# Where the modulation sums accumulate, when the token weights are turned, and when the queue asks for weight slots

## The chip, the core and the metric

The program runs on one NeuronCore of a Trainium2 chip. TensorE (PE in the rows) multiplies, VectorE (DVE), ScalarE (ACT) and GpSimd (POOL) do elementwise work, and SyncE (SP) issues most of the DMAs, one after the other: a DMA whose wait isn't met holds every DMA behind it in that queue. The metric is the device time of one execution, in microseconds, lower is better. Work on the chip is held in SBUF (128 partitions) and in eight PSUM banks of 128 x 512 fp32, which TensorE writes and VectorE and ScalarE may read and write.

## The reference, cut to what matters

A sequence of 512 tokens of width 1024 goes through two layers of a first block and then through a second block of two layers (retention, then differential attention), which the change doesn't touch. One layer of the first block is

```
mod = silu(c) @ w_ada + b_ada               # 6 x 1024: shifts, scales, gates
h   = x * (1 + sc1) + sh1
proj = h @ w_in                             # qa ka va | iq ik iw | cq ckv kr | ga gb
scores[q, s] = sum over 8 heads of iw[q, h] * relu(iq[q, h] . ik[s] / 8), causal
sel  = the 128 best keys of each query by scores
ya   = softmax over sel of (qa . ka / 8 + t5 bias) times va          # "DSA attention"
yb   = causal softmax attention on low-rank q, k, v built from cq, ckv, kr   # "MLA attention"
y    = (sigmoid(ga) * (ya @ w_branch_a) + sigmoid(gb) * (yb @ w_branch_b)) @ w_out
x    = layer_norm(alpha * x + g1 * y); then a gated conv feed-forward, g2, layer_norm
```

Everything is fp32. A projection is three matmuls, with the operands split into a high and a low part (w_hi, w_lo; h_hi, h_lo).

## The kernel before, in words

There is no scheduler: each engine's program is written out by hand, and semaphores order them. Weights come in slots of 128 x 2048 fp32 (1 MB). For slot n, SP loads `w_raw[n % 2]` once slot n-2 has been split (`weights`, L421 to L424), ScalarE rounds it into `w_hi` (`split_hi`, L1141 to L1144), GpSimd subtracts to give `w_lo` (L526, four pieces of 512 columns) and posts `w_ready`. TensorE waits for `w_ready` before the slot's tiles. So SP, ScalarE and GpSimd each pass the slots in order, and a late one delays the rest.

A layer of the first block begins with the index stage. TensorE computes tiles 0 to 7 of the projection (slots 0 to 3: four tiles of iq, then tile 4 with ik, kr and iw, then cq and ckv), turns the 8 x 512 token weights `iw_row` by four small transposes (L792), and goes through twelve pairs of heads (`PAIRS`, L803): two score matmuls (L809) into two of banks 4 to 7, then 15 or 18 matmuls of the gate tiles (`BESIDE[2]`, L601 to L603). ScalarE applies the relu in place (L1320), VectorE adds the two heads into `sel` (L1860, L1863). Pair u's scores wait until VectorE has done pair u-2 (L805). VectorE has other work between: the roots' reciprocals and the norm of cq and ckv (L1866 to L1871), the rotation of kr (L1842 to L1844, after a DMA on SP has swapped its halves, L463), and the modulation sums.

The modulation sums ("ada") are a vector times a matrix. Per layer, 16 slices of w_ada of 1 MB each come through a ring of two buffers `ada_mid`. Slice k is asked for in SP's queue between the weight slots, and its DMA waits until slice k-2 is used up. A number is two slices: eight instructions on VectorE, each one adding a scaled 128 x 512 piece to a sum in SBUF (`ada_acc_early`; L1614 and L1616 in `ada_halves`, L1630 and L1636 in `ada_step_at`). Numbers 4 to 6 stand before the pairs, number 7 to 11 lie in pieces within them (40 steps over 12 pairs). After the fourth tile of the next projection TensorE sums the partitions by 64 one-column matmuls (`ada_group`, L628 to L633).

MLA attention follows: 32 units (4 query blocks x 8 heads) with gate tiles between. VectorE does in each unit a logit pass, a scaling, and some steps of the top-k: a step finds the 8 largest of a row (L1751) and strikes them out (L1752), 16 rounds per query block. Block 1 and 2 (256 and 384 keys) are spread over the units, block 3 (512 keys) runs in a loop (L1738, L1741) after them, under the q, k and v projections (8 tiles and 2 slots). Then VectorE makes `yb_lo` (L1729), which TensorE awaits before DSA attention (L680).

DSA attention has the same 32 units. The bias of unit u, 128 x n, is loaded by SP (L480) once unit u-4's logits are done (four buffers), and between the units TensorE works on the branch tiles (`BESIDE[0]`). The four branch slots 20 to 23 are asked for right behind the biases of units 0 to 3. ScalarE's program is: split slot 20, copy the v tiles, split slot 21 (L1364), then the units' exponentials (L1219).

## Time and profile before

| | |
|---|---|
| median of 3 runs | 2768.3 us (2756.35 to 2777.46) |
| profiled execution | 2764.49 us, span 2762.7 us, mean granted TensorE clock 0.940 |
| PE busy | 2537.8 us, 92% of the span, 11130 matmuls |
| DVE, ACT, POOL busy | 1284.0 (46%), 1085.5 (39%), 1011.0 (37%) us |
| index stage, layer 0 and 1 | 138 to 216 us and 1035 to 1110 us of the span |
| MLA attention with its pairs of tiles | 248 to 338 us and 1143 to 1232 us |
| DSA attention | 404.7 to 498.4 us and 1298.7 to 1407.6 us |

Times within the span count from its start. "Busy" of an engine includes work that runs at the lower of the two clock levels; the granted clock says which (1.00 is 2.4 GHz, 0.50 is 1.2 GHz).

### The profile page before, as it was taken

How to read it: one execution, taken by the hardware profiler on the slowest of the kernel's cores; microseconds unless marked ns; L12 is line 12 of the kernel's file. 1: busy time of each engine (PE TensorE's matmuls, PEld its weight loads, DVE VectorE, ACT ScalarE, POOL GpSimd, SP SyncE). 2: the span in 40 equal slices, each digit the busy share in tenths (PEclk: the TensorE clock that was granted, in tenths of full speed). 3: DMA queues.
4: the chain of work that ended last, by engine and by line, in shares of the span. 5: the costliest groups of instructions: out<-in, count | busy, mean ns of one | idle time of the engine just before them, and what ended most of it. 6: DMA issues, size and time to landing. Idle time of an engine off the chain costs nothing.

```text
span 2762.7 us, 32442 instructions
## 1 busy us (share of the span) xinstructions
PE 2537.8 (92%) x11130; PEld 1959.7 (71%) x11132; DVE 1284.0 (46%) x2520; ACT 1085.5 (39%) x1752; POOL 1011.0 (37%) x792
## 2 busy tenths in 40 slices
PE   6989999889999989999988999997999989799877
PEld 4657875667888866787666788884788768577645
DVE  7675735464435478573356434225310160425472
ACT  5443533354443244443233544324223342323662
POOL 2234240244445553424015344454444434244211
PEclk9998997999999989899588999998999999899988
DMA  6642122112235354213121222222223302122100
GB/s 246 215 174 84 47 83 79 67 61 91 91 102 205 105 196 178 69 47 99 46 69 64 76 105 91 89 94 78 77 90 103 130 1 76 48 89 89 64 1 31
DMA packets 51727, 259.11 MB, mean 94 GB/s; under 512 B 6112, under 2 KB 16096, under 8 KB 26016
## 3 DMA queue, kind: packets, MB, share of 16 engines
q1 hardware_dynamic: 50464, 249.26, 26.2%
q0 software_dynamic: 1152, 8.39, 0.8%
q8 instruction: 67, 1.10, 0.2%
q14 instruction: 44, 0.36, 0.0%
HBM read 249.11 MB, written 7.34 MB: 93 GB/s over the span
## 4 chain that ended last, share of the span: by engine, by line
PE 62%; issue 17%; POOL 8%; DVE 8%; ACT 2%; DMA 2%; SPq 0%; DVEq 0%; POOLq 0%; ACTq 0%
PE bank L601 17%; PE bank L602 17%; PE bank L603 17%; POOL w_lo L526 7%; PE bank L690 2%; PE bank L714 1%; PE bank L998 1%; PE bank L703 1%; PE bank L927 1%; PE bank L632 1%; POOL x L547 1%; DMA ada_early<-w_ada 1%; PE bank L1071 1%; DVE ada_acc_early L1636 1%; DMA ada_mid<-w_ada 1%
## 5 line engine op out<-in xcount | busy, mean ns | idle before, releaser
L526 POOL TENSOR_TENSOR w_lo<-w_raw,w_hi 128x512 fp32r<-128x512 f32 (+1 forms) x700 | 916.5, 1340 | 1491.2 <-ACT w_hi L1144 937.1
L601 PE MATMUL bank<-h_hi,w_hi 128*128 128x512 f32 x1792 | 736.7, 411 | 71.2 <-DVE h_lo L1673 35.3
L603 PE MATMUL bank<-h_hi,w_lo 128*128 128x512 f32 x1792 | 708.6, 395 | 0.0
L602 PE MATMUL bank<-h_lo,w_hi 128*128 128x512 f32 x1792 | 708.2, 395 | 0.0
L601 PEld LDWEIGHTS bank<-h_hi,w_hi 128*128 128x128 f32 x1792 | 343.4, 192 | 173.7 <-issue 85.6
L602 PEld LDWEIGHTS bank<-h_lo,w_hi 128*128 128x128 f32 x1792 | 343.8, 192 | 75.2 <-issue 8.4
L603 PEld LDWEIGHTS bank<-h_hi,w_lo 128*128 128x128 f32 x1792 | 342.4, 191 | 74.1
L1926 DVE SCALAR_TENSOR_TENSOR cv<-bank,par,cv 128x511 f32<-128x511 f32 (+1 forms) x176 | 131.8, 749 | 245.7 <-ACT cv L1389 232.8
L1144 ACT ACTIVATE w_hi<-w_raw 128x2048 fp32r<-128x2048 f32 (+1 forms) x108 | 189.5, 1754 | 135.9 <-PE bank L603 128.6
L1149 ACT ACTIVATE w_hi<-w_raw 128x2048 fp32r<-128x2048 f32 x76 | 145.0, 1907 | 35.8 <-PE bank L603 35.8
L1219 ACT ACTIVATE L<-L,nmax 128x128 f32<-128x128 f32 (+3 forms) x128 | 71.9, 562 | 201.8 <-DVE nmax L1690 201.2
L601 PE MATMUL bank<-u_hi,w_hi 128*128 128x512 f32 x352 | 137.9, 392 | 0.0
L602 PE MATMUL bank<-u_lo,w_hi 128*128 128x512 f32 x352 | 137.0, 389 | 0.0
L603 PE MATMUL bank<-u_hi,w_lo 128*128 128x512 f32 x352 | 137.0, 389 | 0.0
L1389 ACT ACTIVATE cv<-bank,par 128x512 f32<-128x512 f32 x88 | 68.5, 778 | 145.8 <-PE bank L603 145.8
L601 PE MATMUL bank<-w_hi,h_hi 128*128 128x512 f32 x256 | 100.4, 392 | 0.0
L603 PE MATMUL bank<-w_hi,h_lo 128*128 128x512 f32 x256 | 99.6, 389 | 0.0
L602 PE MATMUL bank<-w_lo,h_hi 128*128 128x512 f32 x256 | 99.6, 389 | 0.0
L1687 DVE TENSOR_TENSOR bank<-bank,bias_in 128x128 f32<-128x128 f32 (+3 forms) x64 | 31.9, 498 | 143.7 <-PE bank L690 131.8
L2000 DVE TENSOR_TENSOR wt<-bank,decay 128x512 f32<-128x512 f32 (+3 forms) x32 | 13.5, 482 | 171.8 <-PE bank L987 171.8
L1971 DVE TENSOR_TENSOR rt<-bank,rope 128x512 f32<-128x512 f32 x32 | 22.1, 691 | 127.7 <-PE bank L927 112.5
L1199 ACT ACTIVATE ytmp<-bank,mod 128x512 f32<-128x512 f32 x32 | 22.0, 688 | 147.4 <-PE bank L603 147.4
(322 smaller groups left out, 4005.4 us busy)
## 6 DMA issues: line engine op xcount, KB each, us to landing
w_raw<-w_stream SPq DMA_DIRECT2D x150, 1024.0 KB, 4.8
ada_mid<-w_ada SPq DMA_DIRECT2D x32, 1024.0 KB, 5.5
w_raw<-w_down SPq DMA_DIRECT2D x32, 704.0 KB, 4.0
ada_early<-w_ada POOLq DMA_DIRECT2D x8, 1024.0 KB, 8.4
ada_late<-w_ada SPq DMA_DIRECT2D x8, 1024.0 KB, 6.1
bias_in<-bias_scratch SPq DMA_DIRECT2D x16, 256.0 KB, 2.6
bias_in<-bias_scratch SPq DMA_DIRECT2D x16, 192.0 KB, 2.3
x<-x SPq DMA_DIRECT2D x1, 2048.0 KB, 12.8
```

What stands on the lines that cost most here:

```text
L526: ins = nc.gpsimd.tensor_tensor(w_lo[r][:, part], w_raw[r][:, part], w_hi[r][:, part].bitcast(fp32), ALU.subtract)
L547: nc.gpsimd.tensor_tensor(x[:, f, :], x[:, f, :], ln_mean[:, :], ALU.subtract).then_inc(zs_ready, 1)
L601: nc.tensor.matmul(out, w[0][:, cols], xh, start=first, stop=False)
L602: nc.tensor.matmul(out, w[0][:, cols], xl, start=False, stop=False)
L603: return nc.tensor.matmul(out, w[1][:, cols], xh, start=False, stop=last)
L690: nc.tensor.matmul(banks[4 + t % 2][:, 0:n], q[rows, hh, i * P:(i + 1) * P], kk[rows, hh, 0:n], start=True, stop=True).then_inc(s_done, 1)
L1144: A_(w_hi[n % 2][:, 0:cols], w_raw[n % 2][:, 0:cols], ACT.Copy).then_inc(w_hi_done, 1)
L1149: A_(w_hi[n % 2][:, :], w_raw[n % 2][:, :], ACT.Copy).then_inc(w_hi_done, 1)
L1219: A_(L[t % 3][:, 0:n], L[t % 3][:, 0:n], ACT.Exp, bias=nmax[:, t:t + 1], scale=-1.0, accum_out=esum[:, t:t + 1]).then_inc(exp_done, 1)
L1389: A_(cv[s][c][:, :], banks[(t + c) % 4][:, :], ACT.Identity, bias=b, scale=w2).then_inc(conv_first, 1)
L1687: chain(V.tensor_tensor(ps, ps, bias_in[t % 4][:, 0:n], ALU.add))
L1926: return V.scalar_tensor_tensor(out, banks[(t + c) % 4][:, 0:S - 2 + w], weight, out, ALU.mult, ALU.add)
```

## The change

Four edits, in both layers (the kernel's number for a slot, a slice or a unit is used throughout):

1. The ada sums are built up in a PSUM bank (7 outside the pairs, 3 within them and in the feed-forward of layer 0); the last of the eight instructions writes the total to SBUF. Number 7 moves ahead of the pairs, so 32 steps lie within them. Bank 3 is freed by putting the three root sums into bank 2 one after the other, and TensorE's fourth q tile, which writes bank 3, waits for the last sum. The slices are asked for at other places of SP's queue.
2. The token weights are turned between tiles 5 and 6; the rotation of kr moves behind pair 1, the two reciprocals to pairs 3 and 5, and ScalarE takes a pair's relu before a gate tile's sigmoid.
3. SP asks for the branch slots behind the biases of units 3, 5, 7 and 12 instead of all four behind unit 3's.
4. The top-k of block 2 runs in the loop after MLA attention, ahead of block 3's.

```diff
--- before.py
+++ after.py
@@ -450,7 +450,7 @@
                 for m in range(SLOT_IDX, SLOT_GB + 1):
                     if l or m >= 2:
                         weights(l, m, a["w_ukv"][l] if m == SLOT_UKV else ws[m - (m > SLOT_UKV)])
-                    for _ in range((0, 2, 0, 2, 2, 2, 0, 2, 2, 3, 1)[m]):
+                    for _ in range((0, 2, 0, 1, 2, 3, 1, 2, 2, 2, 1)[m]):
...
@@ -479,9 +479,9 @@
                     n = (i + 1) * P
                     sp.dma_start(bias_in[u % 4][:, 0:n], bias_dram[h, i * P:(i + 1) * P, 0:n]
                                  ).then_inc(bias_full[u % 4], 16)
-                    if u == 3:
-                        for m in range(SLOT_BR, SLOT_OUT):
-                            weights(l, m, ws[m - 1])
+                    if u in (3, 5, 7, 12):
+                        m = SLOT_BR + (3, 5, 7, 12).index(u)
+                        weights(l, m, ws[m - 1])
...
@@ -786,29 +786,35 @@
                 first_slot(l, SLOT_IDX, TILE_IDX, h_hi, h_lo, h_ready, KD * hidx(l, 0))
                 for m in range(1, 4):
                     slot_tiles(l, SLOT_IDX + m, TILE_IDX + 2 * m)
+                    if m == 2:
+                        pe.wait_ge(kr_ready, l + 1)
+                        for b in range(NB):
+                            ins = nc.tensor.transpose(banks[4][:, b * H:(b + 1) * H], iw_row[:, b * P:(b + 1) * P],
+                                                      ident[0:H, 0:H])
+                        ins.then_inc(iw_done, 1)
                 pe.wait_ge(ada_mod, 2 * l + 1)
-                pe.wait_ge(kr_ready, l + 1)
-                for m in range(NB):
-                    ins = nc.tensor.transpose(banks[4][:, m * H:(m + 1) * H], iw_row[:, m * P:(m + 1) * P], ident[0:H, 0:H])
-                ins.then_inc(iw_done, 1)
                 pe.wait_ge(iw_ready, l + 1)
...
-                    nc.tensor.matmul(banks[2 + j // 2][:, :], ones, c_sq[j][:, :], start=(j != 1), stop=(j != 0)
+                    if j == 2:
+                        pe.wait_ge(c_stdd, 2 * l + 1)
+                    nc.tensor.matmul(banks[2][:, :], ones, c_sq[j][:, :], start=(j != 1), stop=(j != 0)
                                      ).then_inc(c_ssq, 1)
...
                 for u, (i, p) in enumerate(PAIRS):
                     n = (i + 1) * P
                     if u >= 2:
                         pe.wait_ge(idx_acc, NI * l + 2 * (u - 1))
+                    if u == 1:
+                        pe.wait_ge(ada_used, 2 * (12 * l + 8))
                     for c in range(2):
                         rows = slice(c * HD, (c + 1) * HD)
                         nc.tensor.matmul(banks[4 + 2 * (u % 2) + c][:, 0:n], iq[rows, p, i * P:(i + 1) * P], ik2[rows, 0:n],
                                          start=True, stop=True).then_inc(idx_s, 1)
-                    if u == 1:
+                    if u == 2:
                         c_squares(2)
...
                     wait_bank(l, TILE_UQ + h, 2 if h < 2 else 4)
+                    if h == 3:
+                        pe.wait_ge(ada_used, 2 * (12 * l + 12))
                     tile(banks[h % 4][:, :], w, h * 2 * P, c_hi, c_lo, 2).then_inc(tile_done, 1)
...
                     tt = ended(2, u - 1)
-                    if tt is not None:
-                        act.wait_ge(tile_done, tdone(l, TILE_GA + tt))
-                        A_(gates[:, tt, :], banks[tt % 2][:, :], ACT.Sigmoid).then_inc(tile_evac, 1)
                     if u < len(PAIRS):
...
                             act.wait_ge(idx_s, NI * l + 2 * u + c + 1)
                             A_(s_, s_, ACT.Relu, scale=HD ** -0.5).then_inc(idx_relu, 1)
                     if u == 1:
+                        act.wait_ge(c_ssq, 3 * l + 2)
+                        A_(c_sq[0][:, :], banks[2][:, :], ACT.Sqrt, bias=rms_eps, scale=1.0 / 256).then_inc(c_stdd, 1)
+                    if u == 2:
                         act.wait_ge(c_ssq, 3 * (l + 1))
-                        A_(c_sq[0][:, :], banks[2][:, :], ACT.Sqrt, bias=rms_eps, scale=1.0 / 256).then_inc(c_stdd, 1)
-                        A_(c_sq[2][:, :], banks[3][:, :], ACT.Sqrt, bias=rms_eps, scale=1.0 / 128).then_inc(c_stdd, 1)
+                        A_(c_sq[2][:, :], banks[2][:, :], ACT.Sqrt, bias=rms_eps, scale=1.0 / 128).then_inc(c_stdd, 1)
+                    if tt is not None:
+                        act.wait_ge(tile_done, tdone(l, TILE_GA + tt))
+                        A_(gates[:, tt, :], banks[tt % 2][:, :], ACT.Sigmoid).then_inc(tile_evac, 1)
...
-            def ada_halves(number, count, late, part):
+            def ada_halves(number, count, late, part, bank):
+                acc = banks[bank][:, :]
                 with dve.Fori(0, count) as it:
-                    acc = ada_acc[late][:, bass.ds(it + part, 1), :].rearrange("p o s -> p (o s)")
+                    total = ada_acc[late][:, bass.ds(it + part, 1), :].rearrange("p o s -> p (o s)")
...
                             if s == 0 and k == 0:
                                 ins = V.tensor_scalar(acc, w, c, None, ALU.mult)
                             else:
-                                ins = V.scalar_tensor_tensor(acc, w, c, acc, ALU.mult, ALU.add)
+                                ins = V.scalar_tensor_tensor(total if s and k == 3 else acc, w, c, acc, ALU.mult, ALU.add)
...
-                acc, w = ada_acc[0][:, part, :], ada_mid[s][:, k * 512:(k + 1) * 512]
+                acc, total, w = banks[3][:, :], ada_acc[0][:, part, :], ada_mid[s][:, k * 512:(k + 1) * 512]
...
-                    ins = V.scalar_tensor_tensor(acc, w, c, acc, ALU.mult, ALU.add)
+                    ins = V.scalar_tensor_tensor(total if s and k == 3 else acc, w, c, acc, ALU.mult, ALU.add)
...
@@ -1647,11 +1658,11 @@
             dve.wait_ge(c_ready, 1)
             steps(0)
             steps(1)
-            ada_halves(0, 1, 0, 0)
+            ada_halves(0, 1, 0, 0, 7)
             steps(2)
-            ada_halves(1, 1, 0, 1)
+            ada_halves(1, 1, 0, 1, 7)
             steps(3)
-            ada_halves(2, 2, 0, 2)
+            ada_halves(2, 2, 0, 2, 7)
...
                     if kind == 1 and t < NU:
-                        rest = [(1, e) for e in range(-1, TOPK // 8 + 1)] + [(2, e) for e in range(-1, TOPK // 8 + 1)]
-                        for i, e in rest[len(rest) * t // NU:len(rest) * (t + 1) // NU]:
-                            topk_step(i, e)
+                        rest = range(-1, TOPK // 8 + 1)
+                        for e in rest[len(rest) * t // NU:len(rest) * (t + 1) // NU]:
+                            topk_step(1, e)
...
             for l in range(DEPTH):
-                ada_halves(12 * l + 4, 2, 0, 0)
+                ada_halves(12 * l + 4, 2, 0, 0, 7)
 
                 dve.wait_ge(tile_done, tdone(l, 4))
                 V.tensor_copy(iw_row[:, :], banks[0][96:96 + H, :])
                 V.tensor_copy(kr_raw[64:96, :], banks[0][64:96, :]).then_inc(kr_ready, 1)
-                ada_halves(12 * l + 6, 1, 0, 2)
-                dve.wait_ge(kr_swapped, 32 * (l + 1))
-                dve.wait_ge(kr_ready, l + 1)
-                chain(V.tensor_tensor(kr_raw[64:96, :], kr_raw[64:96, :], rope[64:96, 0:S], ALU.mult))
-                chain(V.tensor_tensor(kr_swap[64:96, :], kr_swap[64:96, :], rope[64:96, S:2 * S], ALU.mult))
-                V.tensor_tensor(rope[0:32, 0:S], kr_raw[64:96, :], kr_swap[64:96, :], ALU.add).then_inc(kr_turned, 1)
+                ada_halves(12 * l + 6, 1, 0, 2, 7)
                 dve.wait_ge(iw_done, l + 1)
                 V.tensor_scalar(iw_tok[:, :], banks[4][:, 0:32], H ** -0.5, None, ALU.mult).then_inc(iw_ready, 1)
+                ada_halves(12 * l + 7, 1, 0, 3, 7)
...
+                    if u == 1:
+                        dve.wait_ge(kr_swapped, 32 * (l + 1))
+                        dve.wait_ge(kr_ready, l + 1)
+                        chain(V.tensor_tensor(kr_raw[64:96, :], kr_raw[64:96, :], rope[64:96, 0:S], ALU.mult))
+                        chain(V.tensor_tensor(kr_swap[64:96, :], kr_swap[64:96, :], rope[64:96, S:2 * S], ALU.mult))
+                        V.tensor_tensor(rope[0:32, 0:S], kr_raw[64:96, :], kr_swap[64:96, :], ALU.add).then_inc(kr_turned, 1)
+                    if u == 3:
+                        dve.wait_ge(c_stdd, 2 * l + 1)
+                        chain(V.reciprocal(c_sq[0][:, :], c_sq[0][:, :]))
                     if u == 5:
                         dve.wait_ge(c_stdd, 2 * (l + 1))
-                        chain(V.reciprocal(c_sq[0][:, :], c_sq[0][:, :]))
-                    if u == 6:
                         chain(V.reciprocal(c_sq[2][:, :], c_sq[2][:, :]))
                         for j in range(3):
...
-                    for e in range(40 * u // len(PAIRS), 40 * (u + 1) // len(PAIRS)):
-                        ada_step_at(12 * l + 7 + e // 8, 3 + e // 8, e % 8 // 4, e % 4)
+                    for e in range(32 * u // len(PAIRS), 32 * (u + 1) // len(PAIRS)):
+                        ada_step_at(12 * l + 8 + e // 8, 4 + e // 8, e % 8 // 4, e % 4)
...
                 softmax(l, 1)
-                topk_step(3, -1)
-                topk_loop(3, TOPK // 8)
-                topk_step(3, TOPK // 8)
+                for i in (2, 3):
+                    topk_step(i, -1)
+                    topk_loop(i, TOPK // 8)
+                    topk_step(i, TOPK // 8)
                 dve.wait_ge(yt_done, NB * (aidx(l, 1) + 1))
                 for i in range(NB):
                     outputs(1, aidx(l, 1), i, banks[i])
...
                     if l == 0 and f in (0, 1, 2, 5):
-                        ada_halves(12 + min(f, 3), 1, 1, min(f, 3))
+                        ada_halves(12 + min(f, 3), 1, 1, min(f, 3), 3)
```

How it moves rows, at three places. First, SP's queue in the index stage of a layer, from the second ada slice on (`ada_mid_132` and `_133` are the two buffers of the ring, `w_raw_50` and `_51` those of the weights):

```order
 L418 DMA ada_mid_132<-w_ada 128x2048
-L418 DMA ada_mid_133<-w_ada 128x2048
-L424 DMA w_raw_50<-w_stream 128x2048
-L418 DMA ada_mid_132<-w_ada 128x2048
-L418 DMA ada_mid_133<-w_ada 128x2048
-L424 DMA w_raw_51<-w_stream 128x2048
+L424 DMA w_raw_50<-w_stream 128x2048
+L418 DMA ada_mid_133<-w_ada 128x2048
+L418 DMA ada_mid_132<-w_ada 128x2048
+L424 DMA w_raw_51<-w_stream 128x2048
+L418 DMA ada_mid_133<-w_ada 128x2048
```

A slice of the second half of a number, which stood with its first half ahead of a weight slot, now stands behind that slot. The same pattern repeats within the pairs.

Second, SP's queue from the last of the first four biases of DSA attention on (`bias_in_106`, unit 3); biases of units 4 to 7 are 128 wide:

```order
 L480 DMA bias_in_106<-bias_scratch 128x128
 L424 DMA w_raw_50<-w_stream 128x2048
-L424 DMA w_raw_51<-w_stream 128x2048
-L424 DMA w_raw_50<-w_stream 128x2048
-L424 DMA w_raw_51<-w_stream 128x2048
 L480 DMA bias_in_103<-bias_scratch 128x128
 L480 DMA bias_in_104<-bias_scratch 128x128
+L424 DMA w_raw_51<-w_stream 128x2048
 L480 DMA bias_in_105<-bias_scratch 128x128
 L480 DMA bias_in_106<-bias_scratch 128x128
+L424 DMA w_raw_50<-w_stream 128x2048
```

Slot 21 (the first `w_raw_51` here) now stands behind the biases of units 4 and 5, slot 22 behind unit 7's.

Third, VectorE ahead of the first pair, before:

```order
L1838 COPY kr_raw<-bank 32x512
L1602 UNCONDITIONAL_BRANCH
L1614 TENSOR_SCALAR ada_acc_early<-ada_mid_132,csilu 128x512
L1616 SCALAR_TENSOR_TENSOR ada_acc_early<-ada_mid_132,csilu,ada_acc_early 128x512 x3
L1616 SCALAR_TENSOR_TENSOR ada_acc_early<-ada_mid_133,csilu,ada_acc_early 128x512 x4
L1602 REGISTER_ALU
L1602 COMPARE_AND_BRANCH
L1842 TENSOR_TENSOR kr_raw<-kr_raw,rope 32x512
L1843 TENSOR_TENSOR kr_swap<-kr_swap,rope 32x512
L1844 TENSOR_TENSOR rope<-kr_raw,kr_swap 32x512
L1846 TENSOR_SCALAR iw_tok<-bank 128x32
```

and now, from number 6's sum on:

```order
L1627 SCALAR_TENSOR_TENSOR bank<-ada_mid_133,csilu,bank 128x512 x3
L1627 SCALAR_TENSOR_TENSOR ada_acc_early<-ada_mid_133,csilu,bank 128x512
L1613 REGISTER_ALU
L1613 COMPARE_AND_BRANCH
L1852 TENSOR_SCALAR iw_tok<-bank 128x32
L1613 UNCONDITIONAL_BRANCH
L1625 TENSOR_SCALAR bank<-ada_mid_132,csilu 128x512
```

`iw_tok`, which the first pair's scores wait for, no longer stands behind the three kr instructions; number 7 comes behind it.

## Rows read from the trace of the kernel before

**Rows 1.** Stretches: us, busy PE PEld DVE ACT POOL, clock, DMA. DSA attention, two low parts.
```profile
404.70:498.40 93.70, 84.72 (x375) 53.97 (x375) 48.52 (x166) 37.41 (x102) 9.97 (x8) 0.84 0.25 78
1298.70:1407.60 108.90, 101.59 (x375) 64.72 (x374) 48.62 (x166) 37.52 (x102) 9.94 (x8) 0.69 0.22 67
420.30:444.00 23.70, 23.70 (x64) 14.76 (x65) 9.56 (x40) 5.23 (x21) 0.00 (x0) 0.50 0.14 45
1312.80:1376.50 63.70, 63.70 (x181) 40.12 (x181) 23.84 (x86) 16.20 (x50) 4.96 (x4) 0.51 0.15 46
```

**Rows 2.** Waits of TensorE, 93 to 235 us (waiter, releaser: total, times, longest).
```profile
PE bank L809 <- DVE iw_tok L1846: 4.3, 1, 4.3
PE bank L809 <- DVE sel L1863: 3.7, 2, 3.4
PE bank L632 <- DVE ada_acc_early L1636: 1.8, 1, 1.8
```

**Rows 3.** Waits of TensorE, 987 to 1125 us.
```profile
PE bank L809 <- DVE sel L1863: 3.3, 1, 3.3
PE bank L809 <- DVE iw_tok L1846: 2.0, 1, 2.0
PE bank L632 <- DVE ada_acc_early L1636: 1.5, 1, 1.5
```

**Rows 4.** VectorE in order (start, us, ..., [idle before]), ahead of the pairs.
```profile
139.37 0.68 DVE L1842 TENSOR_TENSOR kr_raw<-kr_raw,rope 32x512 f32<-32x512 f32 x1 [5.68 <-DMA kr_swap<-kr_raw]
```

**Rows 5.** SP's queue in order, 128 to 137 us.
```profile
134.09 1.27 SPq L463 DMA_DIRECT2D kr_swap<-kr_raw  x2
```

**Rows 6.** Stretch, first pair.
```profile
142.00:148.00 6.00, 5.28 (x17) 3.83 (x18) 4.01 (x7) 0.68 (x3) 4.04 (x3) 0.72 0.17 30
```

**Rows 7.** VectorE groups by form, 93 to 1130 us (count, busy, mean ns).
```profile
L1636 DVE SCALAR_TENSOR_TENSOR ada_acc_early<-ada_mid,csilu,ada_acc_early 128x512 f32<-128x512 f32 x70 | 66.7, 952 | 3.8 <-DMA ada_mid<-w_ada 1.8
L1863 DVE SCALAR_TENSOR_TENSOR sel<-bank,iw_tok,sel 128x512 f32<-128x512 f32 x14 | 10.5, 748 | 0.8
```

**Rows 8.** Line L418 (ada slices), 93 to 212 us: time from issue to landing.
```profile
DMA to landing us min/median/max: 4.7/5.5/8.6
```

**Rows 9.** VectorE in order, within pair 5.
```profile
177.30 0.49 DVE L1630 TENSOR_SCALAR ada_acc_early<-ada_mid,csilu 128x512 f32<-128x512 f32 x1 [1.64 <-DMA ada_mid<-w_ada]
```

**Rows 10.** TensorE in order, the first partition sums.
```profile
75.37 4.58 PE L632 MATMUL bank<-ck,ada_acc_early 128*128 128x1 f32 x32 [1.06 <-DVE ada_acc_early L1616]
```

**Rows 11.** Stretch of MLA attention, query block 3.
```profile
312.00:334.00 22.00, 22.00 (x134) 17.16 (x133) 17.44 (x58) 10.95 (x26) 0.00 (x0) 1.00 0.01 4
```

**Rows 12.** VectorE in order, from block 3's top-k to `yb_lo`.
```profile
339.05 0.69 DVE L1738 MAX8 top<-sel 128x8 f32<-128x512 f32 x1 [0.30 <-DVE sel L1749]
...
367.90 2.48 DVE L1729 TENSOR_TENSOR yb_lo<-bank,yb_hi 128x512 fp32r<-128x512 f32 x4
```

**Rows 13.** SP's queue in order: slot 21, then unit 4's bias.
```profile
390.61 0.33 SPq L424 DMA_DIRECT2D w_raw<-w_stream  x1
...
412.69 1.54 SPq L480 DMA_DIRECT2D bias_in<-bias_scratch  x3
```

**Rows 14.** Line L424 (weight slots), 360 to 425 us: issue to landing.
```profile
DMA to landing us min/median/max: 4.7/4.8/6.3
```

**Rows 15.** ScalarE in order, split of slot 21 and the exponentials' table.
```profile
405.33 1.90 ACT L1144 ACTIVATE w_hi<-w_raw 128x2048 fp32r<-128x2048 f32 x1
407.25 1.28 ACT L1219 ACT_TABLE_LOAD   x1
```

**Rows 16.** VectorE in order, unit 1's logits.
```profile
407.29 0.29 DVE L1690 CUSTOM_DVE_ANT_0 L<-bank,ck 128x128 f32<-128x128 f32 x1
```

**Rows 17.** TensorE in order, units 2 and 5 of layer 0.
```profile
409.09 0.33 PE L703 MATMUL bank<-ck,L 128*128 128x128 f32 x1 [0.85 <-ACT L L1219]
...
420.30 0.69 PE L714 MATMUL bank<-va,PT 128*128 128x64 f32 x2 [6.11 <-ACT PT L1228]
```

**Rows 18.** TensorE in order, unit 5 of layer 1.
```profile
1312.80 0.69 PE L714 MATMUL bank<-va,PT 128*128 128x64 f32 x2 [4.61 <-ACT PT L1228]
```

## The prediction

> **What bounds the kernel now.** I read the page first: TensorE is busy for 92% of the span, so a step counts only where TensorE waits for it, or where the clock changes. Its stretches [rows 1] show the same DSA attention taking 93.7 us in layer 0 (clock 0.84) and 108.9 in layer 1 (0.69). After one stall in each, TensorE is busy without a gap and yet runs at 1.2 GHz, for 23.7 us in the one, for 63.7 in the other. Then the list of TensorE's waits in the index stage: for `iw_tok` 4.3 and 2.0 us, for `sel` in the pairs 3.7 and 3.3, for the modulation sums 1.8 and 1.5 [rows 2, 3]. Last, the engines' own order around each of these, to see what is late behind them. The sum is made against the profiled execution, 2764.5 us; the median of the runs is 3.8 above it.
>
> **Edit 1, the sums in PSUM.** 64 steps per layer take and give their running sum in a PSUM bank. The trace has no such step, but the nearest has one operand in PSUM: adding a head to `sel` takes 748 ns at the same size, where the ada steps average 952, many of them beside GpSimd's work [rows 7]. So a step costs between 0.75 and 0.95 us; I take 0.75, the nearest row's. Of the 70 steps by 0.20, 14 us of VectorE in both layers, TensorE gets back only what it waited for. That is 1.1 us ahead of the first partition sums [rows 10], and the 1.8 and 1.5 us ahead of the later ones [rows 2, 3], of which I leave 0.5, because q's fourth tile now waits for the last sum one tile ahead of them. Together -1.1 - 2.8 (bounds: none, or -4.4).
>
> The Trainium skill, "VectorE: DVE Perf Modes", section "The TRN2 errata", speaks against this edit: its table has a fixed term of 58 cycles for an SBUF source and 120 for a PSUM source. That is 62 cycles of 0.96 GHz or an estimated 65 ns more per step, 4 us of VectorE per layer. Rows 7 don't show it: the step with a PSUM operand is the shorter one.
>
> **Edit 2, the start of the pairs.** Now `iw_tok` stands behind the rotation of kr, which idles 5.68 us for a DMA [rows 4]. That DMA stands in SP behind number 7's second slice, which waits until VectorE has used number 6's second [rows 5]. With the rotation behind pair 1, `iw_tok` follows number 6's sum at once, at about 134.5, and TensorE wants it at 138.4 (142.7 less the wait). So the waits of 4.3 and 2.0 go, and the 6.0 us at clock 0.72 behind layer 0's [rows 6] give back about 1.5. Against it, TensorE now stops between tiles 5 and 6 for `kr_ready`, which stands on VectorE behind number 5's sum. That number's second slice is asked for one slot later and takes some 5.5 us to land [rows 8], so the sum ends 1 to 2 us later than now: I put 0.4 per layer. Further, pair 1 waits for number 7's sum, whose second slice goes out when number 6 is done, at 134, and lands at 139.6: it ends at 142.6, wanted at 142.5. I put 0.3 per layer. Layer 0: -4.3 - 1.5 + 0.4 + 0.3 = -5.1; layer 1: -2.0 + 0.4 + 0.3 = -1.3. Bounds for both: -7.8 with no new wait, -2 if the new waits are 1 us longer each and the clock gives nothing. The moved rotation is read by MLA attention's first unit, some 90 us on, and its DMA of `km` stands in SP behind the last sum anyway: nothing.
>
> **The pairs.** The wait for `sel` comes from VectorE, which idles for a slice (1.64 us, until 177.30, [rows 9]) and then has the steps, a reciprocal and a norm to do. It now has 32 steps in place of 40 and asks for slices earlier, but number 9's second slice still stands behind slot 8 in SP. It lands at 177.30, less the 5.4 by which the stage runs earlier, less 0.6 since it is alone behind the slot: 171.3. VectorE comes to it, in pair 4, at about 165. Behind it come pair 5's adds (1.3), the reciprocal (3.3), the norm (2.1), four steps (3.1) and pair 6's adds (1.3), so pair 6 is done about 182.5. TensorE's pair 8 wants it at about 178.1, a stall of 4.4 in place of 3.7 and 3.3: +0.7 + 1.1 = +1.8, and its place moves. Bounds: both stalls go (-7.0), or VectorE is 3 us later still (+8).
>
> Up to here: -1.1 - 2.8 - 5.1 - 1.3 + 1.8 = **-8.5**.
>
> **Edit 4, the top-k.** Block 2's rounds leave MLA attention, where TensorE has no gap (22.00 of 22.00, [rows 11]): nothing gained. They stand now in the loop after it. Block 3's loop takes 28.9 us from its first search to `yb_lo` [rows 12]; block 2's is 384 wide instead of 512, so 28.9 at most and about 24.5 by the width. `yb_lo` then ends at 370.4 + 24.5 = 395, and TensorE wants it at 404.7, where DSA attention starts [rows 1]: hidden, with 9 us of slack, or 5 at the upper bound. Cost 0.
>
> **Edit 3, the branch slots.** It takes one stall away and makes another. Now slot 21 is asked for at 390.6 [rows 13] and split by 407.2 [rows 15]. But the biases of units 4 to 6 are held in SP behind slots 22 and 23 and go out only at 412.69 [rows 13], and TensorE waits 6.1 and 4.6 us ahead of unit 5's product [rows 17, 18]. Those waits go: -10.7. In the changed queue slot 21 stands behind unit 5's bias, and that bias waits until unit 1's logits are read, 407.29 + 0.29 [rows 16]. So slot 21 is issued at about 408.0 and lands 4.8 us later [rows 14], at 412.8. ScalarE's program is as it was: it splits slot 21 (1.90 us) and loads its table (1.28) before the first exponential [rows 15]. That one comes at 416.0, TensorE's first transpose at about 416.6 instead of 409.09 [rows 17]: +7.5 per layer, +15.0. From there three units more (2 to 4) run behind the stall; they take 1.4 us each now and would take 2.8 at 1.2 GHz, 4.2 in all if the low stretch is as long behind unit 5 as now, nothing if its total stays. I take half, +2.1 per layer. Sum: -10.7 + 15.0 + 4.2 = **+8.5**. Bounds: -10.7 (the new wait is hidden) and +13 (a longer low stretch in both layers).
>
> **Sum.** -8.5 + 8.5 = 0: 2764.5 by the profile and 2768.3 by the median; I take **2766**. Within 1% (27.7 us) a measurement of this kernel can't tell it from no change, since its three runs lie 21 us apart. The likeliest source of that spread is in rows 1, the length of the low stretch: 12 us lost in layer 0, 32 in layer 1 (half of 23.7 and of 63.7).
>
> **Rivals.**
> (A) The clock comes back sooner. If layer 1 goes as layer 0, 15.2 us are won: 2749. If both come back at once, 44: 2720. I take 2735, chance 0.14. The Trainium skill, "TensorE: Matmul & The Clock Gate", section "What's actually happening", says that activity releases the throttle, by which the dense work behind the stall would run at 2.4 GHz soon. Rows 1 speak against it: 63.7 of 63.7 us busy at clock 0.51.
> (B) No stall in DSA attention at all, because slot 21 arrives ahead of the first exponential's logits. Then the old stalls (10.7) and the low stretches (44) go with the 8.5 of the index stage: 2701. Chance 0.08; rows 14 to 16 speak against it, since the slot can't be asked for before 407.6.
> (C) VectorE isn't starved within the pairs: 1.8 and 7.0 less, 2756. Chance 0.10. For it speak the 8 steps less, against it the slot ahead of the slice.
> (D) Slower: the stall, 7.5 us in place of 6.1 and 4.6, leaves TensorE at 1.2 GHz to the end of the stage in layer 1 (its last 31 us, now at full clock, cost 29 more) and as long as layer 1 in layer 0 (15 more): 2808. It decides once 31 us more are lost to the low clock than now. Chance 0.09; for it speaks that the two stalls of before were followed by such unlike stretches.
> (E) Edit 3 makes no new wait and keeps the old, since unit 4's bias is late for another reason: 2756, chance 0.04.
>
> **Numbers.** The forecast itself has 0.55. (C) and (E) lie in its own range, 2750 to 2785. Left out of 2732 to 2788 are (B), some of (A) and most of (D). Faster by over 1% (below 2740.6): (B) and most of (A), 0.21. Slower (above 2796): (D), 0.09. Between: 0.70.
>
> **What would show it.** In the changed kernel's profile TensorE's wait for `iw_tok` is gone, with small ones between tiles 5 and 6 and at pair 1. VectorE idles for a slice in pair 4 and TensorE waits for `sel` at pair 8. The ada steps take about 0.75 us beside GpSimd too. `yb_lo` is ended by 396. SP issues slot 21 just behind unit 1's logits, ScalarE splits it at about 413, TensorE waits some 7.5 us at unit 2 and not at unit 5, and its clock falls to 0.5 there. I am wrong if TensorE doesn't wait at unit 2, if `yb_lo` comes behind 405, or if the low stretches behind these stalls are together shorter than 60 us or longer than 110.

## The result, and the profile after

The changed kernel takes 2780.2 us (median of 20 runs, 2756.1 to 2792.0), the kernel before 2760.3 (20 runs, 2736.0 to 2781.9): a ratio of 1.0069, interval 1.0046 to 1.0092. It is slower by about 20 us. The ratio leaves out three runs of the kernel before, 2777 to 2782, as slow ones; over all 20 the means lie 16 us apart. I forecast no difference, 2766, so a clear slowdown was missed. The profiled execution takes 2778.8 us, its span 2777.0 against 2762.7. Where these 14.3 us lie, by the starts of the same instructions in both traces (the few us that the medians differ by beyond them aren't located):

| part | before | after | difference |
|---|---|---|---|
| to the first gb tile of MLA attention, layer 0 | 248.24 | 241.75 | -6.5 |
| MLA attention and the q, k, v tiles (each layer) | 156.49 | 156.50 | 0.0 |
| DSA attention to the output projection, layer 0 | 105.40 | 126.27 | +20.9 |
| output projection and feed-forward, layer 0 | 478.80 | 479.83 | +1.0 |
| index stage, layer 1 | 153.30 | 152.16 | -1.1 |
| DSA attention to the output projection, layer 1 | 124.61 | 126.28 | +1.7 |
| the rest | 1339.37 | 1337.71 | -1.7 |

The stretches that answer to [rows 1], by the same columns (us, busy PE PEld DVE ACT POOL, clock, DMA): DSA attention to the output projection in each layer, and inside each the part at the low level.

```profile
398.25:524.52 126.27, 112.28 (x417) 73.49 (x417) 51.39 (x172) 40.62 (x105) 11.14 (x10) 0.70 0.24 73
1313.01:1439.29 126.28, 112.29 (x417) 73.50 (x417) 51.40 (x172) 40.62 (x105) 11.12 (x10) 0.70 0.23 73
411.00:475.00 64.00, 64.00 (x177) 39.83 (x175) 24.33 (x91) 16.56 (x54) 7.38 (x6) 0.50 0.24 76
1325.50:1389.50 64.00, 64.00 (x176) 39.91 (x176) 24.08 (x91) 16.82 (x56) 7.61 (x7) 0.50 0.24 75
```

And the same two stages of the kernel before, which rows 1 show only in part:

```profile
404.73:510.13 105.40, 92.72 (x418) 60.42 (x417) 51.25 (x172) 40.41 (x105) 11.20 (x10) 0.85 0.23 69
1298.72:1423.33 124.61, 113.61 (x418) 74.46 (x417) 51.32 (x172) 40.51 (x105) 11.18 (x10) 0.70 0.19 59
```

Both layers now look as layer 1 did: 64 us at 1.2 GHz, all of them busy. Layer 0 had 26.4 (rows 1 stop at 444.0 with 23.7; the clock rises at 446.7). So of the 20.9 us that layer 0's stage lost, 19.6 are busy time (112.28 against 92.72) and only 1.3 are idle time.

The engines in order around the start of DSA attention, layer 0: SP, then ScalarE, then TensorE (start, us, ..., idle before and its releaser).

```profile
399.44 2.04 SPq L480 DMA_DIRECT2D bias_in<-bias_scratch  x2
401.52 0.43 SPq L424 DMA_DIRECT2D w_raw<-w_stream  x1
402.46 11.29 SPq L480 DMA_DIRECT2D bias_in<-bias_scratch  x2
```

```profile
406.48 1.91 ACT L1152 ACTIVATE w_hi<-w_raw 128x2048 fp32r<-128x2048 f32 x1 [7.53 <-DMA w_raw<-w_stream]
408.41 1.28 ACT L1227 ACT_TABLE_LOAD   x1
```

```profile
410.25 0.47 PE L703 MATMUL bank<-ck,L 128*128 128x128 f32 x1 [8.48 <-ACT L L1227]
410.38 0.77 PE L601 MATMUL bank<-yb_hi,w_hi 128*128 128x512 f32 x1
```

Slot 21 goes out at 401.5, just behind unit 5's bias, ScalarE waits 7.53 us for it with its exponentials behind, and TensorE waits 8.48 us at unit 2 (0.85 stood there before, [rows 17]). The next product takes 0.77 us, where the same one took 0.48 in the kernel before: the clock is at the low level already. In layer 1 the wait is 8.48 as well.

TensorE's waits in the index stage, layer 0 and layer 1, which answer to [rows 2, 3]:

```profile
PE bank L815 <- DVE sel L1870: 5.4, 1, 5.4
PE bank L601 <- DVE ada_acc_early L1647: 3.0, 1, 3.0
PE bank L792 <- DVE kr_raw L1849: 0.4, 1, 0.4
```

```profile
PE bank L815 <- DVE sel L1870: 5.4, 1, 5.4
PE bank L601 <- DVE ada_acc_early L1647: 3.1, 1, 3.1
```

The waits for `iw_tok` are gone, and pair 1's new wait for number 7's sum doesn't appear. The one for `sel` has grown from 3.7 and 3.3 to 5.4, and q's fourth tile waits 3.0 for the last sum. VectorE's order says why (the two places in layer 0 where it idles longest for a slice, with the step behind):

```profile
166.06 0.76 DVE L1647 SCALAR_TENSOR_TENSOR bank<-ada_mid,csilu,bank 128x512 f32<-128x512 f32 x1 [4.96 <-DMA ada_mid<-w_ada]
...
203.80 0.76 DVE L1647 SCALAR_TENSOR_TENSOR bank<-ada_mid,csilu,bank 128x512 f32<-128x512 f32 x1 [7.72 <-DMA ada_mid<-w_ada]
```

The first is number 9's second slice, behind weight slot 8 in SP's queue, in pair 4; the second is number 11's second slice, behind slot 10. Both stood behind these slots in the kernel before too. But there number 11's went out (206.26) as soon as its buffer was free (206.2), 3.2 us behind slot 10. Now its buffer is free at 186.9 and VectorE waits for the slice from 196.1, but slot 10, and the slice behind it, go out only at 196.57 and 196.94. The steps themselves, 93 to 1130 us, by form:

```profile
L1647 DVE SCALAR_TENSOR_TENSOR bank<-ada_mid,csilu,bank 128x512 f32<-128x512 f32 x48 | 36.1, 752 | 29.2 <-DMA ada_mid<-w_ada 28.1
```

They take 752 ns where they took 952 [rows 7], and VectorE idles 29.2 us ahead of them, nearly all for slices, in place of 3.8. And `yb_lo` starts at 383.19:

```profile
383.19 2.48 DVE L1740 TENSOR_TENSOR yb_lo<-bank,yb_hi 128x512 fp32r<-128x512 f32 x4
```

It ends at 385.7, 12.6 us ahead of DSA attention at 398.25.

### The profile page after: what moved, and what is told of

The parts are those of the page before. It is cut to its first block, busy times and chain, and to the rows that moved or that the text cites. A ratio compares the mean times of both kernels' runs of the same rounds, so it can differ in the third digit from the quotient of the medians.

```text
span 2777.0 us, 32642 instructions
## 1 busy us (share of the span) xinstructions
PE 2547.7 (92%) x11132; PEld 1966.6 (71%) x11132; DVE 1245.7 (45%) x2520; ACT 1085.1 (39%) x1752; POOL 993.1 (36%) x792
## 4 chain that ended last, share of the span: by engine, by line
PE 75%; issue 8%; DVE 7%; POOL 4%; ACT 3%; DMA 2%; SPq 0%; DVEq 0%; POOLq 0%; ACTq 0%
PE bank L601 20%; PE bank L603 20%; PE bank L602 20%; POOL w_lo L526 3%; PE bank L690 3%; PE bank L714 3%; PE bank L703 2%; PE bank L1006 1%; DMA ada_mid<-w_ada 1%; PE bank L935 1%; POOL x L547 1%; PE bank L632 1%; PE bank L1079 1%; ACT w_hi L1152 1%; PE bank L995 1%
## 5 line engine op out<-in xcount | busy, mean ns | idle before, releaser
L526 POOL TENSOR_TENSOR w_lo<-w_raw,w_hi 128x512 fp32r<-128x512 f32 (+1 forms) x700 | 898.7, 1315 | 1522.5 <-ACT w_hi L1152 968.3
L703 PEld LDWEIGHTS bank<-ck,L 128*128 128x128 f32 x320 | 41.9, 155 | 70.3 <-issue 42.1
L703 PE MATMUL bank<-ck,L 128*128 128x128 f32 x320 | 67.9, 314 | 17.0 <-ACT L L1227 17.0
```

What stands on the lines that cost most here:

```text
L526: ins = nc.gpsimd.tensor_tensor(w_lo[r][:, part], w_raw[r][:, part], w_hi[r][:, part].bitcast(fp32), ALU.subtract)
L703: ins = nc.tensor.transpose(banks[6 + u % 2][:, b * P:(b + 1) * P], L[u % 3][:, b * P:(b + 1) * P], ident)
```

## The experiments

Each was run with a profile and with the kernel before on the same chip. Ratios are against that kernel, which lay at 2759 to 2763 us throughout.

### What edit 3 does, and what sets off the low clock

**Edit 3 undone** (`a_slots_back`).

```diff
 # after.py, SP
-                    if u in (3, 5, 7, 12):
-                        m = SLOT_BR + (3, 5, 7, 12).index(u)
-                        weights(l, m, ws[m - 1])
+                    if u == 3:
+                        for m in range(SLOT_BR, SLOT_OUT):
+                            weights(l, m, ws[m - 1])
```

> The changed kernel with edit 3 undone: all four branch slots are asked for behind unit 3's bias again. Theory: edit 3 alone makes the change slower, by ScalarE's wait for slot 21 (8.5 us per layer at unit 2) and the longer stretch at 1.2 GHz behind it (64 us in both layers, where layer 0 had 24 before). Then DSA attention is as before and what is left is the index stage's 6.5 and 1.1 us: about 2752, 0.3% below the kernel before. Rival: the loss lies in the other edits (sums in PSUM, top-k), and edit 3 only moved a stall; then it stays near 2780. The waits of 6 and 4.6 us at unit 5 are back in either case.

Measured: 2776.6 us, ratio 1.0058 (1.0022 to 1.0093). My theory asked for 2752 and is refuted as stated: undoing edit 3 gives nearly nothing back, and the time is near the rival's 2780. The waits at unit 5 are back (4.8 and 4.6 us), the 8.5 at unit 2 are gone, and yet both layers have the long stretch:

```profile
397.00:521.62 124.62, 113.47 (x417) 74.43 (x417) 51.34 (x172) 40.48 (x105) 11.16 (x10) 0.70 0.19 59
1315.33:1439.78 124.45, 113.50 (x417) 74.42 (x417) 51.34 (x172) 40.48 (x105) 11.16 (x10) 0.70 0.20 59
```

So with a stall of 4.8 us in layer 0 the stage takes 124.6 us here, where it took 105.4 with one of 6.1 in the kernel before. Layer 0's long stretch (62 busy us at 1.2 GHz) comes without edit 3 too.

**Edit 3 alone** (`b_slots_only`), on the kernel before: the same lines the other way.

> The kernel before with edit 3 alone. Theory: 20 us or more slower than before, about 2787 (the difference of 20 plus the 7.6 us that the index stage gave back): TensorE waits about 8.5 us for the first exponential in both layers, and the clock is at 1.2 GHz for some 64 us behind each. Rival (the loss lies elsewhere, or the length of the low stretch is a matter of chance that edit 3 doesn't touch): 2760 to 2768.

Measured: 2769.4, ratio 1.0051 (1.0027 to 1.0075). Slower, but by 10 and not by 27: nearer the rival's 2768 than the theory's 2787. The waits of 9.0 and 8.4 at unit 2 are there. Its profiled execution (2791.9) is the slowest of 13, with long stretches in both layers; the other twelve lie between 2759 and 2777. Edits 1, 2 and 4 alone cost 17, edit 3 alone 10, all four 20. Costs of work done would add up better than that.

**Slot 21 asked for early** (`c_slot21_early`), the changed kernel otherwise.

```diff
-                    if u in (3, 5, 7, 12):
-                        m = SLOT_BR + (3, 5, 7, 12).index(u)
-                        weights(l, m, ws[m - 1])
+                    for s, at in enumerate((3, 3, 7, 12)):
+                        if u == at:
+                            weights(l, SLOT_BR + s, ws[SLOT_BR + s - 1])
```

> The changed kernel, but slot 21 asked for behind unit 3's bias with slot 20, slots 22 and 23 behind units 7 and 12 as in the change. Theory: neither the wait at unit 2 (slot 21 is there by then) nor the one at unit 5 (unit 4's bias isn't held) is left, and without a stall the clock stays at 2.4 GHz: 2 x 8.5 us of waits and about 2 x 32 us of low clock less than the changed kernel, about 2700. Rival (the low stretch belongs to the small products of DSA attention and not to the stall before it): the waits alone go, 2763.

Measured: 2709.8 (2706.9 to 2718.4), ratio 0.9813 (0.9765 to 0.9860), 70 us below the changed kernel; the theory asked for about 2700, its rival for 2763. The two stages, and TensorE's largest waits for other engines in the first:

```profile
397.02:488.56 91.54, 85.17 (x417) 57.45 (x417) 51.11 (x172) 40.49 (x105) 11.20 (x10) 0.94 0.29 90
1277.60:1369.14 91.54, 85.17 (x417) 57.46 (x417) 51.12 (x172) 40.48 (x105) 11.19 (x10) 0.94 0.29 90
```

```profile
PE bank L714 <- ACT PT L1236: 1.3, 2, 1.1
PE bank L703 <- ACT L L1227: 0.9, 1, 0.9
```

Of the 34.7 us per layer, 7.6 are idle time (14.0 of 126.3 there, 6.4 of 91.5 here) and 27.1 are busy time at the low level (112.3 against 85.2). The stall is the small part of its own price. The 0.94 is one stretch of 10 us at 1.2 GHz at each stage's end, from 469.9 on in layer 0, where a wait of 1.1 us for the last unit stands ahead of it.

**ScalarE splits slot 21 late** (`d_split_late`), SP as in the change.

```diff
                 split_hi(l, SLOT_VA + 2)
...
-                split_hi(l, SLOT_VA + 3)
                 softmax(l, 0)
 # in softmax, behind unit 8's exponential
+                    if kind == 0 and t == 8:
+                        split_hi(l, SLOT_VA + 3)
```

> The changed kernel with SP's queue as it is, but ScalarE splits slot 21 inside the units (behind unit 8's exponential) instead of ahead of the first one. Theory (TensorE waits at unit 2 only because ScalarE's program has the split first): the wait goes although slot 21 lands as late as in the changed kernel, and with it the low stretch: about 2700, like the run with the slot asked for early. Rival (the bias transfers behind the weight slot are what is late): a wait stays at units 2 to 6 and the time near 2775.

Measured: 2764.6, ratio 1.0011 (0.9977 to 1.0044). Half right: the wait at unit 2 is gone, so ScalarE's order was its cause. But slot 23's load now waits in SP for slot 21's buffer, with the biases behind unit 12's behind it, and TensorE stalls at about unit 14, 2.6 us in layer 0 and 3.7 in layer 1. Those small stalls were followed by 30 and 90 busy us at 1.2 GHz.

**A pause and nothing late** (`i_pause_long`). To `c_slot21_early`, ten copies in ScalarE's program, each waiting for the one before.

```diff
+                        if kind == 0 and t == 5:
+                            for q in range(10):
+                                A_(PT[u % 2][:, :], va[:, 0, :], ACT.Copy).then_inc(padded, 1)
+                                act.wait_ge(padded, 10 * l + q + 1)
                         A_(PT[u % 2][:, 0:n], banks[6 + u % 2][:, 0:n], ACT.Copy).then_inc(pt_evac, 1)
```

> c_slot21_early with a pause of ScalarE put into both DSA attention stages: ten copies of 128 x 512, one after the other, ahead of one of the transposed-weight copies (step 5 of the units), an estimated 7 to 8 us by the 0.60 us of such a copy and a wait between. No slot, bias or slice is late in it. Theory (any stall of TensorE in this stage sets off the stretch at 1.2 GHz, whatever causes it): TensorE waits about 7 us once per layer, and behind it come stretches at 1.2 GHz of the two lengths seen (28 us or 62 to 70 us) that cost 14 or 32 us each: between 2710 + 14 + 28 = 2752 and 2710 + 14 + 64 = 2788, with runs in steps of about 18 us. Rival (the late DMAs themselves lower the clock or the pace): the pause alone, 2724.

Measured: 2778.6 (2775.3 to 2782.1), ratio 1.0075 (1.0048 to 1.0103), 69 us above its base. The stall, and the stretch behind it, which is all low:

```profile
411.39 0.69 PE L715 MATMUL bank<-va,PT 128*128 128x64 f32 x2 [6.18 <-ACT PT L1241]
```

```profile
411.40:471.00 59.60, 59.60 (x165) 37.23 (x165) 21.92 (x76) 15.36 (x47) 4.95 (x4) 0.50 0.19 60
```

Two stalls of 6.2 us cost 69, with every slot and bias asked for as in `c_slot21_early`. That is as much as the 70 us between the changed kernel and `c_slot21_early`, made by hand.

**Half the pause** (`j_pause_short`) (five copies).

> The same with five copies, about half the pause. Theory, if any stall of some us sets it off and its length doesn't decide how long the clock stays low: 2710 + 6 + 28 to 64, that is 2744 to 2780, near i_pause_long less 7. Rival (a stall of some 3 us is too short, or the length of the low stretch follows that of the stall): under 2735.

Measured: 2766.9 (2749.7 to 2778.4), ratio 1.0023 (0.9988 to 1.0058). A stall of 2.88 us per layer costs 57 together; in its profile 58 us at the low level follow in both layers (from 411.5 in layer 0, 1 us behind the stall's end). The rival (under 2735, a cost that follows the stall's length) is out.

### What the index stage's edits are worth

From here on the base has no stall in DSA attention, and six runs of a kernel lie within 5 to 12 us of one another, so that 10 us can be read well, and 5 hardly.

**The kernel before with the slots early** (`e_before_early`) (the same edit as in `c_slot21_early`, on before.py).

> The kernel before with the branch slots asked for as in c_slot21_early (slots 20 and 21 behind unit 3's bias, 22 behind unit 7's, 23 behind unit 12's) and nothing else changed. Theory (the stall sets off the low stretch, and without a stall there is none): about 2718, that is 2710 plus the 7.6 us that the changed index stage gained, with a spread of the runs as narrow as there (12 us against 47). Rival (edits 1, 2 and 4 are needed for it): 2745 or more. Against c_slot21_early, it also gives the worth of edits 1, 2 and 4 together, free of the low stretches: 7.6 us by the profile, 0 if the last-sum wait and the longer wait for sel eat it.

Measured: 2715.0 (2708.6 to 2718.7), ratio 0.9822 (0.9777 to 0.9866). The theory holds: the low stretches go without edits 1, 2 and 4. Against 2709.8, these three together are worth 5 us, but the two kernels' runs overlap almost wholly (2706.9 to 2718.4 there), so no more than a few us either way is shown.

**The sums back in SBUF** (`f_sums_sbuf`), on `c_slot21_early` (`acc = total` in both functions).

> c_slot21_early with the ada sums accumulated in SBUF as in the kernel before, everything else left (tables, order, waits). Theory: the steps beside GpSimd's work are 0.2 us and more longer again, so TensorE waits 1 us ahead of the first partition sums, and the waits for sel and for the last sum grow by the few steps behind each late slice, 1 us each: 2710 + 6 = 2716. Rival (what is late is the slice and not the step): 2711. Rival by a longer fixed term for a PSUM source: below 2710.

Measured: 2733.8 (2730.9 to 2738.8), ratio 0.9897 (0.9852 to 0.9941), 24 us above its base where I put 6. The steps, 93 to 235 us:

```profile
L1647 DVE SCALAR_TENSOR_TENSOR ada_acc_early<-ada_mid,csilu,ada_acc_early 128x512 f32<-128x512 f32 x28 | 24.4, 872 | 12.7 <-DMA ada_mid<-w_ada 11.8
L1627 DVE SCALAR_TENSOR_TENSOR ada_acc_early<-ada_mid,csilu,ada_acc_early 128x512 f32<-128x512 f32 x14 | 16.4, 1172 | 3.2 <-DMA ada_mid<-w_ada 2.8
```

Number 7's sum, which edit 1 put ahead of the pairs, is now awaited by pair 1 (3.4 us), and q's fourth tile waits 4.6 us for the last sum.

**The PSUM part of edit 1 alone** (`m_sums_only`), on `e_before_early`: banks 7 and 3 for the sums, bank 2 for the roots, the wait of q's fourth tile; number 7's place, the slices' places, the order and the top-k are those of the kernel before.

> e_before_early with edit 1 alone: the ada sums in PSUM, the three root sums one after the other in bank 2, q's fourth tile waiting for the last sum; the order of VectorE's work, the slices' places in SP's queue, 40 steps in the pairs and block 2's top-k are those of the kernel before. Theory (the steps' 0.2 us is on the path wherever VectorE is late, and each stall costs again in the low clock behind it): the waits before the partition sums go and those for sel shrink, the wait for iw_tok stays, so 8 to 12 us below e_before_early, about 2705, and below c_slot21_early's 2710. That would mean that edit 2 with its slice table costs something. Rival (my prediction's size for edit 1, 3.9 us): 2711. Rival (edit 1 only pays together with number 7 ahead of the pairs): 2715.

Measured: 2695.2 (2692.4 to 2702.3), ratio 0.9759 (0.9706 to 0.9811), 20 us below its base. The sums in PSUM are worth five times my 3.9. In the two profiles, 16.3 of 21.9 us lie ahead of DSA attention in layer 0 (it starts at 389.8 instead of 406.1, at a mean clock of 0.97 instead of 0.95). GpSimd's splits of the weights, in the index stage, without it and with it:

```profile
L526 POOL TENSOR_TENSOR w_lo<-w_raw,w_hi 128x512 fp32r<-128x512 f32 x30 | 46.1, 1566 | 100.5 <-ACT w_hi L1144 100.5
```

```profile
L526 POOL TENSOR_TENSOR w_lo<-w_raw,w_hi 128x512 fp32r<-128x512 f32 x35 | 44.0, 1287 | 96.9 <-ACT w_hi L1150 96.9
```

The relief goes both ways: VectorE's steps fall from 939 to 753 ns and GpSimd's from 1566 to 1287. And the wait for `iw_tok`, which edit 2 was to take away, is 0.5 us here with edit 2 absent (7.6 in the profile of its base).

With `c_slot21_early` these make a table. "New order" is edit 2, number 7's place and the slices' places; edit 4 is in it and is worth nothing (next).

| | order of before | new order |
|---|---|---|
| sums in SBUF | 2715.0 | 2733.8 |
| sums in PSUM | 2695.2 | 2709.8 |

So PSUM gives 20 to 24 us in either order, and the new order costs 15 to 19 with either place of the sums.

**Block 2's top-k back in the units** (`g_topk_units`), on `c_slot21_early`.

> c_slot21_early with block 2's top-k back in the units of MLA attention (edit 4 undone). Theory: TensorE is without a gap there either way and yb_lo has slack either way, so 2710 within 2 us. Rival (its VectorE time in the units delayed MLA attention a little, or the loop's end delays DSA attention): 3 us or more to one side.

Measured: 2712.7 (2706.5 to 2718.0), ratio 0.9816 (0.9772 to 0.9861), against 2709.8 (2706.9 to 2718.4): no difference, as forecast.

**Two slices asked for earlier** (`h_slices_early`), on `c_slot21_early`.

```diff
-                    for _ in range((0, 2, 0, 1, 2, 3, 1, 2, 2, 2, 1)[m]):
+                    for _ in range((0, 2, 0, 1, 2, 3, 1, 3, 2, 2, 0)[m]):
```

> c_slot21_early with two ada slices asked for earlier: number 9's second ahead of weight slot 8 instead of behind it, number 11's second ahead of slot 10. Theory: these two places in SP's queue make VectorE late, so the wait for sel (5.4 us per layer) and the one for the last sum (3.1) go with the low clock behind them (5 to 7 us lost behind the partition sums, 1.4 to 3 behind sel): 2 x 8.5 and about 8 more, about 2685. Rival (VectorE has too much work in pairs 4 to 6, reciprocals and norm, and the slice only fills the gap): 2 to 3 us of sel stay per layer, and 2700.

Measured: 2686.3 (2685.8 to 2690.4), ratio 0.9725 (0.9682 to 0.9769), against 2685 expected. The two slices' places cost more (24 us) than the new order's whole loss of 15, so with them mended it lies 9 us below `m_sums_only`. It is the fastest version here, 2.7% below the kernel before and 3.4% below the changed one. What is left of TensorE's waits for `sel`, layer 0 and layer 1:

```profile
PE bank L815 <- DVE sel L1870: 0.8, 1, 0.8
```

```profile
PE bank L815 <- DVE sel L1870: 2.3, 1, 2.3
```

**The same table on the changed kernel** (`k_change_slices`), edit 3 left in.

> The changed kernel, edit 3 as in the change, with the two slices asked for earlier as in h_slices_early. Theory (the index stage and DSA attention add up): 24 us below the changed kernel, about 2756, since h_slices_early was 24 below c_slot21_early. The wait at unit 2 (8.5 us) and low stretches of about 64 us behind it stay. Rival (how long the low stretch lasts hangs on what went before it, as a_slots_back against the kernel before suggests): 10 us or more off to one side, 2740 or 2772.

Measured: 2740.7 (2726.2 to 2763.4), ratio 0.9947 (0.9911 to 0.9984): 39 below the changed kernel and not 24. The stall at unit 2 is there in full (8.8 and 8.5). In its profile TensorE is busy at 1.2 GHz for 71 us behind the stall of layer 0 and for only 34 behind that of layer 1 (until 1338.8). The rival was right: the savings don't add up, and the length of the low stretch changed with edits that lie ahead of it.

## Why the prediction was wrong, point by point

- **The step that failed is the low clock behind the stall, "+2.1 per layer".** The stall itself came as forecast. Slot 21 went out just behind unit 5's bias and TensorE waited 8.48 us at unit 2, 7.6 more than the 0.85 of before (+7.5 forecast), and not at unit 5. But the +2.1 took for granted that layer 0 keeps its short stretch and layer 1 its long one. In the profiles layer 0's idle time grew by 1.3 us (-6.1 + 7.5 = +1.4 forecast) and its busy time by 19.6 (+2.1 forecast), since 64 us instead of 26 ran at 1.2 GHz: +20.9 for the stage, where the sum had +3.5. Layer 1 had +1.7 (idle +3.0, busy -1.3) where the sum had +5.0. The length isn't a constant of the layer: without edit 3 (`a_slots_back`) layer 0's is long too, and in `k_change_slices` layer 1's is short. Together the two stretches are about 128 us, beyond the 110 that I had named as a sign of being wrong. My rival (D) named it, but only together with a second mishap, at 0.09, and with +15 for layer 0. That is the difference of the parts of the stages in rows 1; the half of 63.7 less 23.7, or the whole stages (124.6 and 105.4), give 19 to 20, which is what came.
- **The same step hides that the stall was the thing to remove.** Rival (B), no stall and so no stretch, was priced at 2701. The kernel with slot 21 early measured 2709.8. The arithmetic was near, and the change misses it by the place of one slot in a queue.
- **The waits before the pairs:** as forecast. `iw_tok`'s are gone, `kr_raw`'s is 0.4 in layer 0 and pair 1's doesn't show (0.4 and 0.3 forecast). The bound of -2 was added wrongly: with each of the four new waits 1 us longer it is -0.9. Nothing hangs on it.
- **The pairs:** a stall of 5.4 us at pair 8 and VectorE idle in pair 4, as forecast, 1.0 us more than the 4.4. It costs more than its length: behind it products take 0.63 us in place of 0.39, until 184.2.
- **The sums in PSUM were sized by the waits they would take away, 3.9 us; by themselves they are worth 20.** I didn't count GpSimd's side, nor that the shorter steps take most of the waits for `iw_tok` and `sel` as well. How the 20 divide isn't shown.
- **The slices' places:** I followed number 9's second slice and not number 11's, which is held by slot 10 now that VectorE is earlier. That made a wait for the last sum of 3.0 and 3.1 us, up from 1.8 and 1.5, where I had -2.8 over both. And the new order as a whole costs 15 us where I had it as a gain of 4.6 (-5.1 - 1.3 + 1.8). This and the sums' size offset one another: that the index stages came out at -7.6 against -8.5 was luck.
- **Edit 4:** 0.0 in both layers, with 12.6 us of slack (9 forecast).
- **The range** (2732 to 2788) holds the 2780, but partly by luck. My upper bound for edit 3 was +13, "a longer low stretch in both layers", and the two stages of DSA attention lost 22.6.

**What stays open.** How long the clock stays low after a stall isn't settled. In the profiles of these kernels, the stretches after a stall in DSA attention ended at unit 12 or 13 (twice: layer 0 of the kernel before, layer 1 of `k_change_slices`), at units 19 to 21 (in all others but one, whether the stall was at unit 2, 5, 6 or 14), or behind the last unit's scores (once, layer 1 of `d_split_late`). So the end goes with the place in the work more than with the stall's length. The times of the kernel before lie around 2740, 2760 and 2780, as two short stretches, one or none would give; most are near 2760. In `a_slots_back`, with a stall in the same place, most are near 2777; in `i_pause_long` all twelve lie between 2775 and 2782, as if the stretch were the long one every time. Why the short stretch is rarer there, no run here shows. So the stall is shown as the cause of the low clock, and the longer stretch of layer 0 as the place of the loss. The choice between the short and the long stretch, on which the 20 us against the kernel before hang, isn't explained.

## What to carry to other kernels

Price a stall of TensorE by the clock behind it, not by its length: here 2.9 us cost 28, and 6.2 cost 34 (per layer, the stall included). When a transfer is moved in a queue, list every engine whose program stands in wait of it, and what that engine would otherwise do first; a load that isn't needed for 14 units may still hold the first one. And compare small edits on a version without the unstable part: 15 and 20 us could be read there, where the runs of a kernel lie 5 to 12 us apart; in the original they lie 46 apart. Compare them one by one, too: here a gain of 20 and a cost of 15 in the same stage looked like a small gain as forecast.

## What the runs showed of the hardware

- Behind every stall of 2.6 us or more in DSA attention, TensorE was at 1.2 GHz for 26 to 90 us while busy almost without a gap. Behind the gaps of 0.4 and 0.9 us among the first units of `c_slot21_early` it stayed at full clock until the last unit. The Trainium skill, "TensorE: Matmul & The Clock Gate", section "What's actually happening", says that activity releases the throttle; in the changed kernel 64.00 of 64.00 us were busy and the clock stayed low.
- A VectorE step whose running sum lies in PSUM took 752 to 756 ns beside GpSimd's work (`c_slot21_early`), in SBUF 818 to 1172 by groups (`f_sums_sbuf`), and GpSimd's own instruction 1287 (`m_sums_only`) in place of 1566 (`e_before_early`). The Trainium skill, "GPSIMD Engine Reference", section "1. Specifications", has GpSimd's SBUF interfaces shared with VectorE where that has two SBUF inputs; the trace agrees. The longer fixed term for a PSUM source, cited in the prediction, doesn't show: in the first 93 us, where GpSimd does only eight such subtractions, the two forms take about the same (752 ns in SBUF in the kernel before, 756 in PSUM in the changed one).
